# Keys and queries of a head requested apart; the feed-forward stage's four weight slots laid over the second mixer's even set and filled during its last head

## The reference, cut to what matters

```python
xn = rms_norm(h, g_attn_pre)
qa, ka, va, qb, kb, vb = split(xn @ w_in)
ya = mixer_a(qa, ka, va)            # grouped-query attention, 8 heads
yb = mixer_b(qb, kb, vb, rel_bias)  # dilated windowed attention, 8 heads of width 64
y = concat([rms_norm(ya, g_out_a), rms_norm(yb, g_out_b)]) @ w_out
h = h + rms_norm(y, g_attn_post)
f = square(relu(rms_norm(h, g_mlp_pre) @ w_ff1)) @ w_ff2
h = h + rms_norm(f, g_mlp_post)
gate = sigmoid(rms_norm(h, g_ple) @ w_ple_gate)
h = h + gate * (p @ w_ple_proj)
```

## Time and profile before

| | |
|---|---|
| median of 3 runs | 3412.59 us (3410.56 to 3412.80) |
| profiled execution, own time | 3412.85 us |
| its span in the profile | 3411.0 us |
| mean granted clock of TensorE | 0.989 |
| PE, PEld busy | 97%, 81% of the span |
| DVE, ACT, POOL busy | 67%, 55%, 54% |
| second mixer | about 1197 to 1592 us from the span's start |
| feed | from 1594 us to the end |

### The profile page before, as it was taken

One profiled execution on the slowest core, in us unless ns is written; L12 is line 12 of the kernel. 1 busy time (PEld: TensorE's weight loads), 2 busy tenths in 40 slices (PEclk: granted clock), 3 DMA queues, 4 the chain that ended last, 5 costly groups with the idle time before them and its releaser, 6 DMA issues.

```text
span 3411.0 us, 48131 instructions
## 1 busy us (share of the span) xinstructions
PE 3303.1 (97%) x17150; PEld 2769.9 (81%) x17150; DVE 2291.7 (67%) x4080; ACT 1860.9 (55%) x3578; POOL 1857.1 (54%) x1434
## 2 busy tenths in 40 slices
PE   8999999999999979998899999999999999999997
PEld 7888878888888769997788887888888888888886
DVE  6465589999999879996556564565645556555554
ACT  3221178888888769997444353344543445443343
POOL 5555534444542168882377732777417775067770
PEclk9999999999999989998999999999999999999998
DMA  5554434445442034434244456444464444744443
GB/s 189 174 172 154 138 128 141 142 144 179 143 166 75 23 88 101 107 84 167 77 137 148 148 197 247 139 152 147 168 237 167 153 147 155 269 142 143 142 138 134
DMA packets 223915, 503.37 MB, mean 148 GB/s; under 512 B 105429, under 2 KB 123421, under 8 KB 204477
## 3 DMA queue, kind: packets, MB, share of 16 engines
q1 hardware_dynamic: 214332, 486.57, 43.1%
q10 hardware_dynamic: 9344, 13.73, 1.1%
HBM read 417.09 MB, written 95.58 MB: 150 GB/s over the span
## 4 chain that ended last, share of the span: by engine, by line
PE 48%; DVE 2%; DMA 1%; ACT 1%; issue 1%; POOL 0%; SPq 0%; DVEq 0%
PE feed_bank L1871 45%; PE feed_bank L1954 1%; PE feed_bank L1862 1%; PE feed_bank L1981 1%; ACT feed_xT L2073 0%; DMA feed_comb<-scr_wG 0%; DMA feed_w_split<-scr_wG 0%; POOL feed_w_split L1827 0%; DMA feed_y_in<-scr_yB 0%; DVE feed_xT L2229 0%; DVE feed_sums L2365 0%; DVE feed_total L2319 0%; ACT feed_w_split L2125 0%; DVE feed_total L2244 0%; DVE feed_ms L2208 0%
## 5 line engine op out<-in xcount | busy, mean ns | idle before, releaser
L1827 POOL TENSOR_TENSOR feed_w_split<-feed_w_raw,feed_w_split 128x1024 fp32r<-128x1024 f32 x352 | 882.4, 2517 | 249.2 <-ACT feed_w_split L2125 236.0
L1871 PE MATMUL feed_bank<-feed_w_split,feed_comb 128*128 128x512 f32 x3552 | 821.8, 391 | 16.7 <-DVE feed_sums L2365 7.8
L1871 PEld LDWEIGHTS feed_bank<-feed_w_split,feed_comb 128*128 128x128 f32 x3552 | 664.5, 188 | 162.4 <-POOL feed_w_split L1827 11.8
L1871 PE MATMUL feed_bank<-feed_xT,feed_w_split 128*128 128x512 f32 x3072 | 701.0, 390 | 2.6 <-DVE feed_xT L2229 2.6
L1871 PEld LDWEIGHTS feed_bank<-feed_xT,feed_w_split 128*128 128x128 f32 x3072 | 577.7, 188 | 123.4 <-DVE feed_xT L2229 3.0
L1110 DVE TENSOR_TENSOR mixa_pT<-mixa_turned,mixa_pT 128x512 fp32r<-128x512 f32 x512 | 351.2, 686 | 58.9 <-ACT mixa_pT L1052 52.6
L1824 POOL TENSOR_SCALAR feed_w_split<-feed_w_raw 128x1024 fp32r<-128x1024 f32 x128 | 136.6, 1067 | 464.1 <-PE feed_bank L1871 285.0
L1052 ACT ACTIVATE mixa_pT<-mixa_turned 128x512 fp32r<-128x512 f32 x512 | 307.2, 600 | 118.1 <-PE mixa_turned L988 99.3
L933 PE MATMUL mixa_out_acc<-mixa_pT,mixa_v_hl 128*128 128x512 f32 x1028 | 365.7, 437 | 0.2
L2140 ACT ACTIVATE feed_rl<-feed_bank 128x512 f32<-128x512 f32 x128 | 76.5, 598 | 523.6 <-PE feed_bank L1871 523.6
L2319 DVE TENSOR_TENSOR feed_total<-feed_total,feed_bank 128x512 f32<-128x512 f32 x352 | 224.5, 682 | 195.5 <-PE feed_bank L1871 192.6
(11 more groups left out here) (211 smaller groups left out, 5447.2 us busy)
## 6 DMA issues: line engine op xcount, KB each, us to landing
feed_w_raw<-scr_wT SPq DMA_DIRECT2D x160, 512.0 KB, 3.3
feed_w_split<-scr_wG SPq DMA_DIRECT2D x68, 1024.0 KB, 4.9
feed_w_raw<-w_tail_dram SPq DMA_DIRECT2D x128, 512.0 KB, 3.5
proj_w_raw<-w_in_dram SPq DMA_DIRECT2D x36, 1024.0 KB, 5.3
feed_w_raw<-w_ff_dram SPq DMA_DIRECT2D x64, 512.0 KB, 3.4
scr_table<-scr_bias SPq DMA_DIRECT2D x8, 1520.0 KB, 8.7
scr_wG<-mixb_q_in SPq DMA_DIRECT2D x9, 1024.0 KB, 3.9
scr_wG<-mixb_k_in SPq DMA_DIRECT2D x9, 1024.0 KB, 7.0
```

Source lines behind the costliest of these rows:

```text
L1827: pool.tensor_tensor(w_sp[slot][:, 1, :], w_raw[:, slot, :], w_sp[slot][:, 0, :].bitcast(F32), ALU.subtract).then_inc(w_lo, 1)
L1871: mm = pe.matmul(dst, lhs, rhs, start=start, stop=stop)
```

## The change

1. The semaphore `qk_dma` becomes two, `k_dma` and `q_dma`, each with two DMAs per head; `load_qk` becomes `load_k` and `load_q`. For head 1 the keys are requested once five pieces of head 0 are split, the queries once all eight are. POOL waits for `k_dma` before its first piece of keys and for `q_dma` before its first piece of queries.
2. The four weight slots are no longer tiles of their own. `v_hl[0]`, `qT[0]` and the high part `kT[0][0]` are allocated on the right side by the feed inputs and stay; the slots are two halves of `v_hl[0]`, all of `qT[0]` and the first 2048 columns of `kT[0][0]`. Their first contents are requested in the last head (which uses set 1), once the value products of the seventh head are done (`pv_done`).
3. Feed therefore starts with `w_far`, followed by `res`. The two semaphores of the h2 store and reload become one with counts 16 and 32.

```diff
-    def load_qk(self, sp, h):
+    def load_k(self, sp, h):
...
+    def load_q(self, sp, h):
...
+    def load_first(self, sp, scr, C):
+        sp.dma_start(self.w_sp[C].bitcast(F32), scr["wG"][C]).then_inc(self.w_dma[C], 16)
...
-            next_qk(0, 1)
+            sp.wait_ge(pre_lo, len(FIRST_ORDER))
+            heads.load_k(sp, 1)
+            sp.wait_ge(pre_lo, PRE)
+            heads.load_q(sp, 1)
             next_v(0, 1)
...
             feed.load_consts(sp, *consts)
+            sp.wait_ge(pv_done, (NHB - 1) * NU)
+            for C in range(NSPL4):
+                feed.load_first(sp, scr, C)
             store(NHB - 1, 0)
...
                 if m == 4:
-                    pool.wait_ge(qk_dma, h * (16 * QK_DMAS) + 16 * QK_DMAS)
+                    pool.wait_ge(k_dma, h * (16 * K_DMAS) + 16 * K_DMAS)
                     pool.wait_ge(sc_done, (h - 1) * NU + 2)
+                if m == 0:
+                    pool.wait_ge(q_dma, h * (16 * Q_DMAS) + 16 * Q_DMAS)
...
-            for C in range(NSPL4):
-                load_split(C, C, C)
-            for t in range(TT):
-                sp.dma_start(res[:, t, :], x[t * P:(t + 1) * P, :]).then_inc(x_dma[t], 16)
             for q in range(NR4):
                 sp.wait_ge(w_dma[q], 16)
                 sp.dma_start(w_far[q].bitcast(F32), scr["wG"][NR4 + q]).then_inc(w_dma[q], 16)
+            for t in range(TT):
+                sp.dma_start(res[:, t, :], x[t * P:(t + 1) * P, :]).then_inc(x_dma[t], 16)
```

More of the change, by code:

```diff
@@ L73 @@
     VT = NU + RES * RES
-    QK_DMAS, V_DMAS = 4, 1 + 2 * RES * (RES - 1)
+    K_DMAS, Q_DMAS, V_DMAS = 2, 2, 1 + 2 * RES * (RES - 1)
     def __init__(self, nc, ctx, scr):
@@ L83, in __init__ @@
         self.t_own = [k.sb(f"t_own{u}", [P, 7 * P]) for u in range(2)]
-        self.qk_dma, self.v_dma, self.t_dma = k.sem("qk_dma"), k.sem("v_dma"), k.sem("t_dma")
-    def load_qk(self, sp, h):
[L87 to L90, removed]
+        self.k_dma, self.q_dma, self.v_dma, self.t_dma = (k.sem(n) for n in ("k_dma", "q_dma", "v_dma", "t_dma"))
+    def load_k(self, sp, h):
+        for twice in range(2):
+            sp.dma_start(self.k_in[twice * HD:(twice + 1) * HD, :], self.scr["kBT"][bass.ds(h * HD, HD), :]
+                         ).then_inc(self.k_dma, 16)
+    def load_q(self, sp, h):
+        for twice in range(2):
+            sp.dma_start(self.q_in[twice * HD:(twice + 1) * HD, :], self.scr["qBT"][bass.ds(h * HD, HD), :]
+                         ).then_inc(self.q_dma, 16)
     def load_v(self, sp, h):
@@ L127, in __init__ @@
         k = Kit(nc, ctx, "feed")
+        self.v_hl = k.sb("v_hl0", [P, HeadInputs.VT, 2 * HD], F32R, side="right")
+        self.qT = k.sb("qT0", [P, S], F32R, side="right")
+        self.kT = k.sb("kT0", [P, S + 2 * PAD], F32R, side="right")
+        self.w_sp = [a.rearrange("p (h c) -> p h c", h=2) for a in
+                     (self.v_hl[:, 0:16, :].rearrange("p n c -> p (n c)"),
+                      self.v_hl[:, 16:32, :].rearrange("p n c -> p (n c)"), self.qT[:], self.kT[:, 0:2 * self.CW])]
         self.total = k.sb("total", [P, TT, D], side="right")
@@ L778, in _ @@
             sp.wait_ge(wt_out, T_OUT + 32 * BATCHES)
-            heads.load_qk(sp, 0)
+            heads.load_k(sp, 0)
+            heads.load_q(sp, 0)
             heads.load_near(sp, 0)
@@ L1144, in mixer_b_phase @@
         q_in, k_in, v_in, t_near, t_own = heads.q_in, heads.k_in, heads.v_in, heads.t_near, heads.t_own
-        kT = [[k.sb(f"kT{u}{h}", [P, SW], F32R) for h in range(2)] for u in range(2)]
-        qT = [k.sb(f"qT{u}", [P, S], F32R) for u in range(2)]
-        v_hl = [k.sb(f"v_hl{u}", [P, VT, 2 * HD], F32R) for u in range(2)]
+        kT = [[feed.kT, k.sb("kT01", [P, SW], F32R)], [k.sb(f"kT1{h}", [P, SW], F32R) for h in range(2)]]
+        qT = [feed.qT, k.sb("qT1", [P, S], F32R)]
+        v_hl = [feed.v_hl, k.sb("v_hl1", [P, VT, 2 * HD], F32R)]
         t_oth = [k.sb(f"t_oth{u}", [P, 6, P]) for u in range(2)]
@@ L1166, in mixer_b_phase @@
         set_done = k.sem("set_done")
-        qk_dma, v_dma, t_dma = heads.qk_dma, heads.v_dma, heads.t_dma
+        k_dma, q_dma, v_dma, t_dma = heads.k_dma, heads.q_dma, heads.v_dma, heads.t_dma
         t_done_pool = k.sem("t_done_pool")
@@ L1174, in mixer_b_phase @@
         y_out = k.sems("y_out", 2)
-        QK_DMAS, V_DMAS = heads.QK_DMAS, heads.V_DMAS
+        K_DMAS, Q_DMAS, V_DMAS = heads.K_DMAS, heads.Q_DMAS, heads.V_DMAS
         T_COPIES = 2 + 6 * (RES - 1)
@@ L1192, in next_qk @@
                 sp.wait_ge(pre_lo, h * PRE + PRE)
-                heads.load_qk(sp, nxt)
+                heads.load_k(sp, nxt)
+                heads.load_q(sp, nxt)
             def next_v(h, nxt):
@@ L1242, in _ @@
             sp.wait_ge(t_dma, 32 * NHB)
-            sp.wait_ge(qk_dma, 16 * QK_DMAS * NHB)
+            sp.wait_ge(k_dma, 16 * K_DMAS * NHB)
+            sp.wait_ge(q_dma, 16 * Q_DMAS * NHB)
             sp.wait_ge(v_dma, 16 * V_DMAS * NHB)
@@ L1653, in feed_phase @@
         w_raw = k.sb("w_raw", [P, NR4, CW])
-        w_sp = [k.sb(f"w_split{i}", [P, 2, CW], F32R) for i in range(NSPL4)]
+        w_sp = feed.w_sp
         res = k.sb("res", [P, TT, D])
@@ L1742, in load_split @@
             def load_split(C, j, slot):
-                if not (isinstance(C, int) and C < NSPL4):
-                    sp.wait_ge(w_used, C - NSPL4 + 2)
+                sp.wait_ge(w_used, C - NSPL4 + 2)
                 sp.dma_start(w_sp[slot][:].bitcast(F32), scr["wG"][j]).then_inc(w_dma[slot], 16)
```

16 lines of the change are left out of this document (8 added, 8 removed).

## The result

| kernel | median us | runs | ratio to the kernel before, 95% interval |
|---|---|---|---|
| before | 3412.48 (3410.56 to 3412.80) | 4 | |
| after | 3435.53 (3434.11 to 3437.19) | 4 | 1.0068 [1.0054, 1.0082] |

The prediction was 3392.0 with a range of 3387 to 3399, and 0.03 for "slower". The changed kernel is 0.7% slower, and its time lies 43.5 us above the forecast. The profiled execution of the changed kernel took 3437.19, its span is 3435.4.

A forecast was written before the change was run, and what follows sets the result against it. The prediction took the kernel to be bound by PE, busy 97% of the span. Profiled 3412.85 us less 13.1 (earlier keys) less 7.6 (earlier slot fill) gave 3392.1, stated as 3392.0, range 3387 to 3399.

The forecast's parts named there:

- slower than before: Feed: slots at new, scattered addresses slow each weight load or product; placement costs 0.05, of which 0.03 clearly slower.
- the example: Feed: at 4.2 ns more per product the kernel would be 7 us slower, 3419 us.
- the break-even: Feed: 3.1 ns more per product, 0.8% of 390 ns, would use up the predicted 20.7 us.
- The count of 6624: Feed: the 3552 + 3072 products of L1871 taken as those the new slot addresses could slow.
- the two gains: 13.1 us from earlier keys in the second mixer and 7.6 us at feed's start, 20.7 us together.
- Part 1: Second mixer, head 0: requesting head 1's keys earlier removes PE's 11.7 us wait and slow clock after it, gaining 13.1 us.
- the copies and tables behind them: Head 0: 24 small copies done 4 to 6 us sooner, tables issued near 1233, landed 1238, 1 us before need.
- the wait moves: Head 0: queries or bias tables come late instead, costing 1 to 3.8 us, up to 3396; chance 0.08.
- that term: Head 0: POOL's and then PE's loss to late tables, bounded by 0 and 3.8 us, taken as 0.
- Part 2: Start of feed: filling slots in the last head lets the pieces over comb land earlier, gaining 7.6 us.
- The fill's cost: Last head: four SP issues and 4 MB ahead of the store, which lands near 1569 with 10 us cover; cost 0.
- The sum: Whole kernel: profiled 3412.85 less 13.1 less 7.6 gives 3392.1, stated as 3392.0 us.

The follow-up runs named there:

- its run alone: Kernel before plus only the slots filled in the last head, started at multiples of 256 bytes; keys and queries requested together as before: 3406.49 us, ratio 0.9979.
- the well placed one: Changed kernel with 224 bytes left free ahead of the slots and 128 more ahead of kT, so slots start at multiples of 256: 3393.98 us, ratio 0.9939.

## Why the prediction was wrong

**The step that failed** is the one that set aside the rival "slower than before". Its mechanism, slots at new addresses that slow each product of feed, is what happened; its size was 5.9 ns a product, where the example had 4.2 and the break-even 3.1. The count of 6624 was short as well: the products of L1871 with a slot moving over `xT`, 576 of them, and the 96 of L1981 are missing, and with all 7296 the two gains are used up at 2.8 ns. It was given 0.05 on one argument: `comb` and the slots lie far apart and have medians of 390 and 389. That comparison varied the distance and kept fixed what matters: `comb`, `xT` and the four old slots all start at multiples of 256. Two rows can only speak against a cause if the cause differs between them. The starts after the change were not looked up, although an allocation shows them before anything runs. With them, 224 and 96 against 0 would at least have made this an untested case rather than an argued one.

The trace of the kernel before held a second clue, which I had not read. In its projection stage every tile of the products starts 224 past a multiple of 256 (by the allocation, `xT` at 54496, 70880 and 87264, `w_split` at 128224 and 144608), and their median is 389 ns all the same:

```profile
L429 PE MATMUL proj_bank<-proj_xT,proj_w_split x512: 388/389/501, 54.0 to 409.3; 128*128 128x512 f32 x171
```

Read beside the slots of the changed kernel at 224, this row alone rules out that a start of 224 costs by itself.

**Part 1** was right in its mechanism and 1 us too large in what reaches feed: the keys' wait is gone, and 13.2 us are gained at N = 3 against 13.1. What was said of the copies and tables behind them was half right. The 24 copies of the values took 18.46 us, not some 15, and the tables were issued at 1235.66, not near 1233; these are SP and POOL in head 0 of the changed kernel:

```profile
1202.32 1.09 SPq L88 DMA_DIRECT2D mixb_k_in<-scr_kBT  x2
1215.34 1.08 SPq L93 DMA_DIRECT2D mixb_q_in<-scr_qBT  x2
...
1217.10 18.46 SPq L106 DMA_DIRECT2D mixb_v_in<-scr_vB  x24
1235.66 0.38 SPq L113 DMA_DIRECT2D mixb_t_near<-scr_table  x1
```

```profile
1241.48 0.96 POOL L1287 COPY mixb_t_oth<-mixb_t_near 128x384 f32<-128x384 f32 x2 [2.12 <-DMA mixb_t_own<-scr_table]
```

POOL waited 2.12 us for the second table, and PE 0.99 for POOL, the row at 1243.86 above. The rival "the wait moves" was thus true as well, for 1 us of its 0 to 3.8. I had put that term at 0 by the estimate that an emptier queue would hurry the copies by 4 to 6 us; they took 1.7 us less. That a full queue holds up the first copy was my reading. Measured is that it held SP for 9.41 us in the kernel before, with the DMA engines at a mean share of 1.05 from 1218 to 1228, and for 6.38 in the changed one, at 0.74; the other 23 took 12.08 us instead of 10.78.

**Part 2** was right in kind and size, as its run alone shows: 7.55 us at the place, 7.9 in the medians. In the changed kernel itself it looks smaller, since the 24 slot products of the first set took 8.44 us from 1590.69 to 1599.13, against 7.71 before; they start at the lower clock (granted 0.50 from 1592 to 1596) and differ from kernel to kernel (7.23 in the well placed one, 1592.01 to 1599.24, granted 0.55 over the same stretch).

**The fill's cost** was nothing, and near the forecast. The four transfers were issued from 1541.05 on, and `load_y`, which waits for the store behind them, went out at 1557.30: 16.3 us after the first issue, where the forecast has 1569 less 1553, 16. No new wait of POOL or PE followed. The store did feel the transfers: from its issue to that of `load_y` it is 7.59 us, where the kernel before has 1.97 (1561.79 to 1563.76). The four landed 7.4 to 14.2 us after their issues, the last near 1557.0, and the store near 1557.3, 7.6 us after its own issue, where the kernel before has 2.0: behind all four, and all within 16.3 us of the first issue. That it had to land behind them, no run shows. SP, last head:

```profile
1541.05 0.91 SPq L151 DMA_DIRECT2D feed_v_hl<-scr_wG  x2
1541.99 0.72 SPq L151 DMA_DIRECT2D feed_qT<-scr_wG  x1
1542.75 0.64 SPq L151 DMA_DIRECT2D feed_kT<-scr_wG  x1
1549.71 0.37 SPq L1223 DMA_DIRECT2D scr_yB<-mixb_y_st  x1
1557.30 0.32 SPq L154 DMA_DIRECT2D feed_total<-scr_yA  x1
```

**The sum** was sound to 2 us apart from the missing term: 3392.0 predicted, 3393.98 measured once the term is taken out; against the kernel before, measured beside it, that is a gain of 20.4 where the prediction has 20.7. That it comes so close is in part luck, since part 1 brought 1 us less to feed than predicted.

## What to carry to other kernels

When a change moves a tile that PE reads, write down where it starts and where its partners start, modulo 256, before and after; 6 ns a product is invisible in any one row and 43 us in a stage of 7300 products. After any change of the layout, compare the median duration of the products, not only the waits. And when a row is used against a rival, ask first whether the two cases that it compares differ in the very thing that the rival names.

## What the hardware showed

For products of 128x128 by 128x512 in fp32r, at a granted clock of 1.00 from 1800 to 3300 in every run, medians in ns by the difference of the operands' starts modulo 256 (the shorter way round, both roles, groups of over 500 products):

| difference | 0 | 16 | 32 | 64 | 96 | 128 |
|---|---|---|---|---|---|---|
| medians | 389 | 389 and 394 | 394 to 396 | 392 to 394 | 394 to 397 | 393 to 395 |

The weight loads have medians of 187 or 188 ns in all of them; over the whole span PE's busy time grows from 3303.1 to 3348.6 us and PEld's does not. The 128x256 products of the second mixer with `v_hl` show no such loss. Their partner `pT` starts at 0 in the kernel before and at 128 in the changed one, so with `v_hl` at 0 and then at 224 the difference goes from 0 to 96; the mean is 292 ns in both:

```profile
L1419 PE MATMUL mixb_out_acc<-mixb_pT,mixb_v_hl 128*128 128x256 f32 x960 | 144.8, 292 | 4.3 <-ACT mixb_y_part L1486 1.0
```

```profile
L1443 PE MATMUL mixb_out_acc<-mixb_pT,feed_v_hl 128*128 128x256 f32 x480 | 72.4, 292 | 2.1 <-ACT mixb_y_part L1510 0.3
```

The difference of two starts thus has a price in time, 43 us of 3412.

What stays open is the cause inside the chip, which no run shows. Open too are why 16 costs with the shifted operand moving and not with it held (with one role changed the sign of the difference changes too, and no run parts the two), why the other remainders differ among themselves by 2 ns, why the 128x256 products are spared, and whether other data types behave so. The difference of 16 was seen in one kernel, each of the others in two or more, with one profiled run of each kernel.
